# Splitting weights on GpSimd in smaller instructions, in one inference step of a diffusion backbone

## The chip, the cores and the metric

The kernel runs on one core of a Trainium2 chip. The metric is device time of one execution in microseconds, as the median over runs.

## What is computed

One step of a two-layer backbone over 128 context tokens and 512 latent tokens, 1024 channels, all in float32, with one set of weights. Cut to what matters here:

```python
def trunk(x, cond, states, is_context):
    for layer in range(DEPTH):                      # DEPTH = 2
        mod = jax.nn.silu(cond) @ w_ada[layer] + b_ada[layer]
        shift1, scale1, gate1, shift2, scale2, gate2 = jnp.split(mod[:, None, :], 6, axis=-1)
        h = rmsnorm(x, norm_mix_g[layer]) * (1 + scale1) + shift1
        if layer % 2 == 0:
            y, s_fin = mixer_ab(h, ...)             # gated DeltaNet || short gated conv, then @ w_out
        else:
            y = multiscale_pool(h, w_pool[o], pool_scale[o])
        x = x + gate1 * y
        h = rmsnorm(x, norm_ffn_g[layer]) * (1 + scale2) + shift2
        x = x + gate2 * conv_ffn(h, w_ffn_gate[layer], w_ffn_up[layer], ffn_conv[layer], w_ffn_down[layer])
    return rmsnorm(x, final_norm_g), finals

def conv_ffn(h, w_gate, w_up, conv, w_down):        # D_FF = 2816
    u = dwconv3(h @ w_gate, conv)
    return (jax.nn.silu(u) * (h @ w_up)) @ w_down
```

## The kernel before

All 640 tokens lie along the free axis and channels along the 128 partitions. A matrix product is done in units: one unit makes 128 output channels for all tokens, with 8 weight tiles of 128 x 128 (7 where a down group has 7 tiles of the hidden width, so 1024 or 896 columns of weights). Each float32 operand is split in a rounded part and a rest (`hi`, `lo`), and a unit multiplies three products, hi x hi, hi x lo and lo x hi, in 48 (or 42) matmuls of 320 columns (`products`, L942).

The weights of a unit arrive by DMA in `raw[s]`, s being the unit's number modulo 2. They are split in `whi[s]` (L758, a `tensor_scalar` by 1.0 plus 0.0 with rounded output) and `wlo[s]` (L761, a `tensor_tensor` subtraction, `raw` less `whi`). `split` does both on GpSimd: it waits for the load (`s_raw`) and until unit u - 2 is multiplied (`s_unit`), so it begins when TensorE turns to unit u - 1, and it tells TensorE by `s_split`. In the input projection VectorE and ScalarE split instead; in the up units of the first layer ScalarE rounds (L2094) and GpSimd only subtracts (`split_lo`, L766). The same two instructions stand written out for some units with buffers of their own: `first_hi`/`first_lo` (L864, L866), `third_hi`/`third_lo` (L897, L899), `mid_hi`/`mid_lo` (L853, L855), `last_hi`/`last_lo` (L910, L913). SyncE loads `raw[s]` again once `s_split` says that the unit in it is split.

The program goes: input projection (28 units), the DeltaNet scans, output projection (8 units), then for each layer three groups of the FFN, each with pairs of up units (gate and up, 8, 7 and 7 pairs) and 8 down units. The pooling mixer stands between the layers.

VectorE's work beside this is what the prediction speaks of. After an up pair's first unit, ScalarE copies the product (L2103), VectorE scales it (L2233) and adds two taps of the convolution in two ranges each (L2236, L2242); ScalarE applies silu (L2110); VectorE multiplies by the second unit's product, which it reads from PSUM (L2897); ScalarE rounds to `hidhi`, and VectorE subtracts to `hidlo` (L2900). In the down units and in the output projection VectorE updates x from PSUM (L2178, L2189) and, in the latter, adds squares (L2156). In between, in the first layer, in the output projection and in the second layer's first up group, it works off the modulation weights, rows of `w_ada`, two sums of 1024 columns for each row tile (`row_sums`, L2219; the tile `ada_raw`, outputs `junk` and `ada_raw`). TensorE waits for `hidlo` before a group's first down unit reaches the tile in question, and for the update of x before a pair of PSUM banks is written again.

The down group at the end of each layer is done in two halves of the tokens (L1392, L1523), with weights kept for both.

Of the kernel before, what the change touches and what calls it, by code (L numbers as in the profile page):

```python
# [61 lines left out]
SLOT = KD * P  # L62
PRIMED = 4

F32 = mybir.dt.float32
F32R = mybir.dt.float32r
ALU = mybir.AluOpType
# [90 lines left out]
def build(nc, t):  # L158
    ctx = ExitStack()
    with ctx:  # L160
# [9 lines left out]
        raw = [sb(f"raw{s}", [P, SLOT]) for s in range(2)]  # L170
# [579 lines left out]

        @block.gpsimd
        def _(pool):
            def split(u, half_u, s, n=SLOT, guard=True):
                pool.wait_ge(s_raw[s], half_u * 16 + 16)
                if guard:
                    pool.wait_ge(s_unit, u - 1)
                pool.sem_inc(s_go, 1)
                nc.gpsimd.tensor_scalar(whi[s][:, 0:n], raw[s][:, 0:n], 1.0, 0.0,  # L758
                                        ALU.mult, ALU.add).then_inc(s_whi, 1)
                pool.wait_ge(s_whi, u + 1)  # L760
                nc.gpsimd.tensor_tensor(wlo[s][:, 0:n], raw[s][:, 0:n], whi[s][:, 0:n].bitcast(F32),  # L761
                                        ALU.subtract).then_inc(s_split, 1)

            def split_lo(u, s):
                pool.wait_ge(s_whi, u + 1)
                nc.gpsimd.tensor_tensor(wlo[s][:], raw[s][:], whi[s][:].bitcast(F32),  # L766
                                        ALU.subtract).then_inc(s_split, 1)

            def split_lo_pairs(u, n_pairs, first=0):
                with pool.Fori(first, n_pairs) as i:  # L770
# [79 lines left out]
            def mid_split(m):  # L850

                pool.wait_ge(s_mid_raw[m], 16)
                nc.gpsimd.tensor_scalar(mid_hi[m][:], mid_raw[m][:], 1.0, 0.0, ALU.mult, ALU.add).then_inc(s_kept_hi, 1)  # L853
                pool.wait_ge(s_kept_hi, m - 1)
                nc.gpsimd.tensor_tensor(mid_lo[m][:], mid_raw[m][:], mid_hi[m][:].bitcast(F32),  # L855
                                        ALU.subtract).then_inc(s_kept_w, 1)

            for g, nf in enumerate(GROUPS):
                if g == 0:
                    u = SEG["up", 0, 0]["u"]  # L860
                    for j in range(2):
                        pool.wait_ge(s_raw[j], u // 2 * 16 + 16)
                        pool.wait_ge(s_unit, SEG["out"]["u"] + 2)
                        nc.gpsimd.tensor_scalar(first_hi[j][:], raw[j][:], 1.0, 0.0, ALU.mult, ALU.add).then_inc(s_whi, 1)  # L864
                        pool.wait_ge(s_whi, u + j + 1)
                        nc.gpsimd.tensor_tensor(first_lo[j][:], raw[j][:], first_hi[j][:].bitcast(F32),  # L866
                                                ALU.subtract).then_inc(s_split, 1)
                else:
                    split_pairs(SEG["up", 0, g]["u"], 1)
                if g == 2:  # L870
                    mid_split(2)
                u = SEG["up", 0, g]["u"] + 2
                if g == 0:
                    pool.wait_ge(s_raw[0], u // 2 * 16 + 16)
                    pool.wait_ge(s_unit, SEG["out"]["u"] + 7)
                    nc.gpsimd.tensor_scalar(whi[0][:], raw[0][:], 1.0, 0.0, ALU.mult, ALU.add).then_inc(s_whi, 1)
                    split_lo(u, 0)
                    split_lo(u + 1, 1)
                split_lo_pairs(u, nf, int(g == 0))
                if g < 2:  # L880
                    split_pairs(SEG["down", 0, g]["u"], 4, nf * P, first=1)
# [10 lines left out]
            for g, nf in enumerate(GROUPS[:2]):  # L892
                u = SEG["up", 1, g]["u"]
                if g == 0:
                    split_pairs(u, 1)
                    pool.wait_ge(s_raw[0], (u + 2) // 2 * 16 + 16)
                    nc.gpsimd.tensor_scalar(third_hi[:], raw[0][:], 1.0, 0.0, ALU.mult, ALU.add).then_inc(s_whi, 1)  # L897
                    pool.wait_ge(s_whi, u + 3)
                    nc.gpsimd.tensor_tensor(third_lo[:], raw[0][:], third_hi[:].bitcast(F32),  # L899
                                            ALU.subtract).then_inc(s_split, 1)  # L900
                    split(u + 3, (u + 2) // 2, 1)
                    split_pairs(u, nf, first=2)
                else:
                    split_pairs(u, nf)
                split_pairs(SEG["down", 1, g]["u"], 4, nf * P)

            def last_split(j):

                pool.wait_ge(s_last_raw, 16 * (KD - 2))
                nc.gpsimd.tensor_scalar(last_hi[j][:], last_raw[j - 2][:], 1.0, 0.0, ALU.mult, ALU.add)\  # L910
                    .then_inc(s_kept_hi, 1)
                pool.wait_ge(s_kept_hi, KEPT + j - 1)
                nc.gpsimd.tensor_tensor(last_lo[j][:], last_raw[j - 2][:], last_hi[j][:].bitcast(F32),  # L913
                                        ALU.subtract).then_inc(s_kept_w, 1)

            u = SEG["up", 1, 2]["u"]
            split_pairs(u, 3)
# [2179 lines left out]
```

## Time and profile before

| | |
|---|---|
| median of 3 runs | 1422.23 us (1421.07 to 1422.54) |
| the profiled execution | 1421.06 us |
| its span | 1419.3 us |
| TensorE (PE) busy | 1366.4 us, 96% |
| VectorE (DVE) busy | 989.5 us, 70% |
| ScalarE (ACT) busy | 412.9 us, 29% |
| GpSimd (POOL) busy | 517.7 us, 36% |
| GpSimd, L761 | 89 instructions, 229.4 us |
| GpSimd, L766 | 44 instructions, 112.5 us |
| GpSimd, L758 | 89 instructions, 95.8 us |

The span goes from the first to the last instruction. An instruction's time in a timeline runs from when its engine begins it to its end, and time in which it is held back inside counts as busy. So equal shapes with unequal durations are worth a look, and a busy share is not a share of work.

### The profile page before, as it was taken

The page shows a single profiled execution, that of the slowest core. Times are in us where ns is not written, and L with a number is a line of the kernel's source. Part 1 is how long each engine was busy: PE and PEld are TensorE (multiplying, and loading weights), DVE is VectorE, ACT ScalarE, POOL GpSimd, SP SyncE. Part 2 cuts the span into 40 slices and gives each one's busy share as a digit, 9 for nine tenths or more (in the row PEclk, how much of TensorE's full clock was granted, in tenths as well). Part 3 has the DMA queues.
Part 4 walks back from the last instruction along what each step waited for, and adds up shares of the span by engine and source line. Part 5 has one row for each costly group of instructions (what it writes and reads, how often), then busy time and mean ns, then how long its engine had stood idle before and what let it go on. Part 6 is the DMA issues. An engine that isn't in the chain of part 4 may idle for free.

```text
span 1419.3 us, 23699 instructions
## 1 busy us (share of the span) xinstructions
PE 1366.4 (96%) x9266; PEld 1331.6 (94%) x9266; DVE 989.5 (70%) x1474; ACT 412.9 (29%) x752; POOL 517.7 (36%) x315
## 2 busy tenths in 40 slices
PE   6999999989888999999999999999999999999997
PEld 4899899989778999999999999989999999999997
DVE  4887889858777877877788885688881355235554
ACT  4535344656026331023202232561110011001122
POOL 0000200141451334633465336215544455456650
PEclk9999999999999999999999999999999999999999
DMA  9645113432341453343354432112322224222202
GB/s 370 259 163 164 45 60 105 157 105 76 104 148 45 133 194 136 135 149 118 126 182 134 149 119 74 53 37 101 121 86 74 74 74 148 78 75 74 72 14 75
DMA packets 44718, 163.48 MB, mean 115 GB/s; under 512 B 4848, under 2 KB 7536, under 8 KB 42608
## 3 DMA queue, kind: packets, MB, share of 16 engines
q1 hardware_dynamic: 44656, 162.66, 33.1%
q8 instruction: 38, 0.62, 0.2%
q14 instruction: 24, 0.20, 0.0%
HBM read 154.26 MB, written 6.82 MB: 113 GB/s over the span
## 4 chain that ended last, share of the span: by engine, by line
PE 69%; DVE 13%; issue 10%; ACT 5%; POOL 2%; DMA 0%; DVEq 0%; ACTq 0%; SPq 0%; POOLq 0%
PE ps L942 52%; PE ps L1523 3%; PE ps L1392 3%; DVE junk L2219 2%; POOL wlo L766 2%; DVE ada_raw L2219 2%; DVE work L2236 1%; PE ps L1462 1%; PE ps L954 1%; DVE blocks L2435 1%; DVE outer L2432 1%; ACT work L1965 1%; PE ps L992 1%; PE ps L1086 1%; PE ps L1327 1%
## 5 line engine op out<-in xcount | busy, mean ns | idle before, releaser
L942 PE MATMUL ps<-hhi,whi 128*128 128x320 f32 x1824 | 419.3, 311 | 8.0 <-DVE x L2189 5.2
L942 PE MATMUL ps<-hlo,whi 128*128 128x320 f32 x1824 | 416.0, 309 | 0.0
L942 PE MATMUL ps<-hhi,wlo 128*128 128x320 f32 x1824 | 415.9, 309 | 0.0
L942 PEld LDWEIGHTS ps<-hhi,whi 128*128 128x128 f32 x1824 | 305.5, 188 | 12.2 <-DVE x L2189 6.0
L942 PEld LDWEIGHTS ps<-hlo,whi 128*128 128x128 f32 x1824 | 305.8, 188 | 0.0
L942 PEld LDWEIGHTS ps<-hhi,wlo 128*128 128x128 f32 x1824 | 305.7, 188 | 0.0
L761 POOL TENSOR_TENSOR wlo<-raw,whi 128x1024 fp32r<-128x1024 f32 (+1 forms) x89 | 229.4, 2578 | 7.4
L758 POOL TENSOR_SCALAR whi<-raw 128x1024 fp32r<-128x1024 f32 (+1 forms) x89 | 95.8, 1076 | 346.6 <-PE ps L942 272.6
L766 POOL TENSOR_TENSOR wlo<-raw,whi 128x1024 fp32r<-128x1024 f32 x44 | 112.5, 2558 | 208.7 <-ACT whi L2094 208.7
L2103 ACT ACTIVATE work<-ps 128x640 f32<-128x640 f32 x44 | 31.0, 704 | 380.3 <-PE ps L942 378.5
L2219 DVE SCALAR_TENSOR_TENSOR ada_raw<-ada_raw,cond_rows 128x1024 bf16<-128x1024 f32 x80 | 137.4, 1717 | 0.0
L2900 DVE TENSOR_TENSOR hidlo<-work,hidhi 128x640 fp32r<-128x640 f32 (+1 forms) x44 | 95.8, 2178 | 43.0 <-ACT hidhi L2115 43.0
L2219 DVE SCALAR_TENSOR_TENSOR junk<-ada_raw,cond_rows 128x1024 bf16<-128x1024 f32 x80 | 117.3, 1467 | 3.4 <-DMA ada_raw<-in_w_rows 1.0
L942 PE MATMUL ps<-hidhi,whi 128*128 128x320 f32 x480 | 110.1, 311 | 2.1 <-DVE hidlo L2900 2.1
L2236 DVE SCALAR_TENSOR_TENSOR work<-work,cols 128x511 f32<-128x511 f32 x120 | 109.3, 952 | 3.7 <-DVE work L2233 0.5
L2233 DVE TENSOR_SCALAR work<-work,cols 128x640 f32<-128x640 f32 x60 | 60.2, 1003 | 73.7 <-ACT work L2103 69.0
L942 PE MATMUL ps<-hidlo,whi 128*128 128x320 f32 x480 | 109.9, 310 | 0.0
L942 PE MATMUL ps<-hidhi,wlo 128*128 128x320 f32 x480 | 109.9, 310 | 0.0
L2110 ACT ACTIVATE work<-work 128x640 f32<-128x640 f32 x44 | 32.5, 739 | 265.5 <-DVE work L2242 265.5
L942 PEld LDWEIGHTS ps<-hidhi,whi 128*128 128x128 f32 x480 | 80.9, 189 | 2.4 <-DVE hidlo L2900 2.4
L942 PEld LDWEIGHTS ps<-hidlo,whi 128*128 128x128 f32 x480 | 80.9, 189 | 0.0
L942 PEld LDWEIGHTS ps<-hidhi,wlo 128*128 128x128 f32 x480 | 80.9, 189 | 0.0
(323 smaller groups left out, 1854.3 us busy)
## 6 DMA issues: line engine op xcount, KB each, us to landing
raw<-in_w_gu SPq DMA_DIRECT2D x88, 512.0 KB, 3.3
ada_raw<-in_w_rows SPq DMA_DIRECT2D x80, 512.0 KB, 3.4
raw<-in_w_in SPq DMA_DIRECT2D x28, 512.0 KB, 3.3
raw<-in_w_dn SPq DMA_DIRECT2D x24, 448.0 KB, 3.3
ada_first<-in_w_ada SPq DMA_DIRECT2D x8, 1024.0 KB, 18.3
raw<-in_w_dn SPq DMA_DIRECT2D x16, 512.0 KB, 3.5
raw<-in_w_out SPq DMA_DIRECT2D x8, 512.0 KB, 3.3
last_raw<-in_w_dn SPq DMA_DIRECT2D x6, 448.0 KB, 6.7
```

The costliest lines, as they stand in the source:

```text
L758: nc.gpsimd.tensor_scalar(whi[s][:, 0:n], raw[s][:, 0:n], 1.0, 0.0, ALU.mult, ALU.add).then_inc(s_whi, 1)
L761: nc.gpsimd.tensor_tensor(wlo[s][:, 0:n], raw[s][:, 0:n], whi[s][:, 0:n].bitcast(F32), ALU.subtract).then_inc(s_split, 1)
L766: nc.gpsimd.tensor_tensor(wlo[s][:], raw[s][:], whi[s][:].bitcast(F32), ALU.subtract).then_inc(s_split, 1)
L942: last = nc.tensor.matmul(pair[pr][:, b], wt[:, cs], act[:, k, b * HALF:(b + 1) * HALF], start=(first and j == 0 and q == 0), stop=(final ...
L1392: last = nc.tensor.matmul(mid_out(i)[:, 0:MID_SPANS[b][1] - MID_SPANS[b][0]], wt[:, cs], mid_of(act[:, j], b), start=(j == 0 and q == 0), ...
L1523: last = nc.tensor.matmul(pair["CB"[i % 2]][:, i // 2 % 2], wt[m][:, cs], half_of(act[:, j], b), start=(j == 0 and q == 0), stop=(j == LAS ...
L2103: nc.scalar.activation(halves(pad[0]), pair["A"], ACT.Copy).then_inc(s_ev["A"], 1)
L2110: nc.scalar.activation(cv[1], cv[0], ACT.Silu).then_inc(s_silu, 1)
L2219: last = nc.vector.scalar_tensor_tensor(out=(row_out(n), row_buf(n)[:, 0:SLOT // 2].bitcast(mybir.dt.bfloat16))[c], in0=row_buf(n), scalar ...
L2233: own.tick(nc.vector.tensor_scalar(dst[:, 0:W], src[:, 0:W], taps[1], None, ALU.mult))
L2236: last = nc.vector.scalar_tensor_tensor(out=dst[:, c0 + 1:c0 + n], in0=src[:, c0:c0 + n - 1], scalar=taps[0], in1=dst[:, c0 + 1:c0 + n], o ...
L2900: nc.vector.tensor_tensor(hidlo[:, i, :], h32[0], hidhi[:, i, :].bitcast(F32), ALU.subtract).then_inc(s_hid, 1)
```

## The change

Every rounding of weights on GpSimd is issued as two instructions over half the columns, and every subtraction as four over a quarter. The semaphore is raised by the last of them. Waits, buffers, the order of the work and all other engines stay as they are.

```diff
+            def round_parts(dst, src, n):
+
+                for c in range(0, n, n // 2):
+                    last = nc.gpsimd.tensor_scalar(dst[:, c:c + n // 2], src[:, c:c + n // 2], 1.0, 0.0, ALU.mult, ALU.add)
+                return last
+
+            def rest_parts(dst, src, hi, n):
+
+                for c in range(0, n, n // 4):
+                    cs = slice(c, c + n // 4)
+                    last = nc.gpsimd.tensor_tensor(dst[:, cs], src[:, cs], hi[:, cs].bitcast(F32), ALU.subtract)
+                return last
+
             def split(u, half_u, s, n=SLOT, guard=True):
                 pool.wait_ge(s_raw[s], half_u * 16 + 16)
                 if guard:
                     pool.wait_ge(s_unit, u - 1)
                 pool.sem_inc(s_go, 1)
-                nc.gpsimd.tensor_scalar(whi[s][:, 0:n], raw[s][:, 0:n], 1.0, 0.0,
-                                        ALU.mult, ALU.add).then_inc(s_whi, 1)
+                round_parts(whi[s], raw[s], n).then_inc(s_whi, 1)
                 pool.wait_ge(s_whi, u + 1)
-                nc.gpsimd.tensor_tensor(wlo[s][:, 0:n], raw[s][:, 0:n], whi[s][:, 0:n].bitcast(F32),
-                                        ALU.subtract).then_inc(s_split, 1)
+                rest_parts(wlo[s], raw[s], whi[s], n).then_inc(s_split, 1)
 
             def split_lo(u, s):
                 pool.wait_ge(s_whi, u + 1)
-                nc.gpsimd.tensor_tensor(wlo[s][:], raw[s][:], whi[s][:].bitcast(F32),
-                                        ALU.subtract).then_inc(s_split, 1)
+                rest_parts(wlo[s], raw[s], whi[s], SLOT).then_inc(s_split, 1)
...
```

The six places that have the instructions written out (L853 to L913) change in the same way.

On GpSimd, the loop over down units of 896 columns, before:

```order
L758 TENSOR_SCALAR whi<-raw 128x896
L760 REGISTER_ALU
L761 TENSOR_TENSOR wlo<-raw,whi 128x896
L756 REGISTER_ALU
L758 TENSOR_SCALAR whi<-raw 128x896
L760 REGISTER_ALU
L761 TENSOR_TENSOR wlo<-raw,whi 128x896
```

and with the change, whose lines are numbered anew:

```order
L756 TENSOR_SCALAR whi<-raw 128x448 x2
L772 REGISTER_ALU
L763 TENSOR_TENSOR wlo<-raw,whi 128x224 x4
L769 REGISTER_ALU
L756 TENSOR_SCALAR whi<-raw 128x448 x2
L772 REGISTER_ALU
L763 TENSOR_TENSOR wlo<-raw,whi 128x224 x4
```

Nothing moves: each instruction becomes two or four in its place, with nothing between the parts. The other engines' rows are the same but for their line numbers.

## Rows read from the trace of the kernel before

**Rows 1.** Table by stages: length; busy PE, PEld, DVE, ACT, POOL (count); clock; DMA.

```profile
445.00:848.00 403.00, 402.91 (x2745) 402.73 (x2746) 330.82 (x394) 88.04 (x109) 178.46 (x77) 1.00 0.41 140
```

**Rows 2.** Timeline of TensorE: start, us, what; in brackets idle before, and for whom.

```profile
366.36 0.41 PE L942 MATMUL ps<-hhi,whi 128*128 128x320 f32 x1 [0.35 <-POOL wlo L761]
...
408.06 0.39 PE L1327 MATMUL ps<-hhi,whi 128*128 128x320 f32 x1 [3.75 <-DVE x L2189]
...
850.43 0.42 PE L1392 MATMUL ps<-hidhi,whi 128*128 128x336 f32 x1 [0.85 <-POOL wlo L766]
...
931.80 0.33 PE L1438 MATMUL ps<-band,rows_tok 128*128 128x112 f32 x1 [0.86 <-DVE x L2807]
...
1060.05 0.47 PE L942 MATMUL ps<-hidhi,whi 128*128 128x320 f32 x1 [2.12 <-DVE hidlo L2900]
...
1361.78 0.41 PE L1523 MATMUL ps<-hidhi,whi 128*128 128x320 f32 x1 [0.73 <-POOL wlo L761]
```

**Rows 3.** Timelines: a GpSimd subtraction, a sum held by it, a sum alone.

```profile
367.89 3.24 POOL L761 TENSOR_TENSOR wlo<-raw,whi 128x1024 fp32r<-128x1024 f32 x1
...
368.81 3.41 DVE L2219 SCALAR_TENSOR_TENSOR ada_raw<-ada_raw,cond_rows 128x1024 bf16<-128x1024 f32 x1
...
1049.91 1.22 DVE L2219 SCALAR_TENSOR_TENSOR ada_raw<-ada_raw,cond_rows 128x1024 bf16<-128x1024 f32 x1
```

**Rows 4.** GpSimd with nobody in its way: timeline, and a group of lines (mean ns).

```profile
384.51 2.41 POOL L761 TENSOR_TENSOR wlo<-raw,whi 128x1024 fp32r<-128x1024 f32 x1
...
L913 POOL TENSOR_TENSOR last_lo<-last_raw,last_hi 128x896 fp32r<-128x896 f32 x6 | 12.8, 2128 | 0.5
...
1133.33 1.05 POOL L758 TENSOR_SCALAR whi<-raw 128x1024 fp32r<-128x1024 f32 x1 [3.49 <-PE ps L942]
...
1358.60 0.94 POOL L758 TENSOR_SCALAR whi<-raw 128x896 fp32r<-128x896 f32 x1 [3.64 <-issue]
```

**Rows 5.** Timelines about 279.8 us: a GpSimd row of small instructions, a VectorE copy.

```profile
277.72 2.45 POOL L807 TENSOR_SCALAR kg_p<-ktok,gates 128x128 f32<-128x128 f32 x7 [2.63 <-ACT ktok L1721]
...
279.81 0.64 DVE L2447 COPY work<-blocks 32x512 f32<-32x512 f32 x1
...
280.15 0.53 POOL L807 TENSOR_SCALAR kg_p<-ktok,gates 128x128 f32<-128x128 f32 x1
...
279.80 0.37 POOL L807 TENSOR_SCALAR kg_p<-ktok,gates 128x128 f32<-128x128 f32 x1
```

**Rows 6.** Timelines of one down unit of 896 columns, first layer.

```profile
723.82 0.94 POOL L758 TENSOR_SCALAR whi<-raw 128x896 fp32r<-128x896 f32 x1 [2.07 <-PE ps L942]
724.84 3.07 POOL L761 TENSOR_TENSOR wlo<-raw,whi 128x896 fp32r<-128x896 f32 x1
...
729.82 1.14 DVE L2189 SCALAR_TENSOR_TENSOR x<-ps,mod,x 128x320 f32<-128x320 f32 x3 [0.82 <-PE ps L942]
```

**Rows 7.** Timeline of VectorE at the end of the output projection.

```profile
403.48 3.37 DVE L2219 SCALAR_TENSOR_TENSOR ada_raw<-ada_raw,cond_rows 128x1024 bf16<-128x1024 f32 x1
```

**Rows 8.** Table by stages again, behind two waits of TensorE: the clock follows POOL.

```profile
375.80:379.20 3.40, 3.38 (x23) 3.39 (x24) 2.54 (x2) 0.74 (x1) 2.27 (x1) 1.00 0.57 178
...
1060.30:1063.70 3.40, 3.40 (x14) 3.40 (x14) 2.87 (x5) 0.00 (x0) 1.56 (x2) 0.50 0.00 0
```

**Rows 9.** Timeline of GpSimd in the pooling mixer.

```profile
921.33 2.36 POOL L899 TENSOR_TENSOR third_lo<-raw,third_hi 128x1024 fp32r<-128x1024 f32 x1
```

**Rows 10.** Timeline of VectorE in a pair of the second layer's first up group.

```profile
1045.10 1.55 DVE L2900 TENSOR_TENSOR hidlo<-work,hidhi 128x640 fp32r<-128x640 f32 x1 [0.90 <-ACT hidhi L2115]
1046.57 3.41 DVE L2219 SCALAR_TENSOR_TENSOR junk<-ada_raw,cond_rows 128x1024 bf16<-128x1024 f32 x1
...
1051.63 1.80 DVE L2236 SCALAR_TENSOR_TENSOR work<-work,cols 128x511 f32<-128x511 f32 x2
1053.46 2.85 DVE L2242 SCALAR_TENSOR_TENSOR work<-work,cols 128x511 f32<-128x511 f32 x1
```

**Rows 11.** Timeline of GpSimd before the last down projection.

```profile
1359.62 2.10 POOL L761 TENSOR_TENSOR wlo<-raw,whi 128x896 fp32r<-128x896 f32 x1
```

More of the change, by code:

```diff
@@ L852, in mid_split @@
                 pool.wait_ge(s_mid_raw[m], 16)
-                nc.gpsimd.tensor_scalar(mid_hi[m][:], mid_raw[m][:], 1.0, 0.0, ALU.mult, ALU.add).then_inc(s_kept_hi, 1)
+                round_parts(mid_hi[m], mid_raw[m], LAST).then_inc(s_kept_hi, 1)
                 pool.wait_ge(s_kept_hi, m - 1)
-                nc.gpsimd.tensor_tensor(mid_lo[m][:], mid_raw[m][:], mid_hi[m][:].bitcast(F32),
-                                        ALU.subtract).then_inc(s_kept_w, 1)
+                rest_parts(mid_lo[m], mid_raw[m], mid_hi[m], LAST).then_inc(s_kept_w, 1)
             for g, nf in enumerate(GROUPS):
@@ L863, in _ @@
                         pool.wait_ge(s_unit, SEG["out"]["u"] + 2)
-                        nc.gpsimd.tensor_scalar(first_hi[j][:], raw[j][:], 1.0, 0.0, ALU.mult, ALU.add).then_inc(s_whi, 1)
+                        round_parts(first_hi[j], raw[j], SLOT).then_inc(s_whi, 1)
                         pool.wait_ge(s_whi, u + j + 1)
-                        nc.gpsimd.tensor_tensor(first_lo[j][:], raw[j][:], first_hi[j][:].bitcast(F32),
-                                                ALU.subtract).then_inc(s_split, 1)
+                        rest_parts(first_lo[j], raw[j], first_hi[j], SLOT).then_inc(s_split, 1)
                 else:
@@ L875, in _ @@
                     pool.wait_ge(s_unit, SEG["out"]["u"] + 7)
-                    nc.gpsimd.tensor_scalar(whi[0][:], raw[0][:], 1.0, 0.0, ALU.mult, ALU.add).then_inc(s_whi, 1)
+                    round_parts(whi[0], raw[0], SLOT).then_inc(s_whi, 1)
                     split_lo(u, 0)
@@ L896, in _ @@
                     pool.wait_ge(s_raw[0], (u + 2) // 2 * 16 + 16)
-                    nc.gpsimd.tensor_scalar(third_hi[:], raw[0][:], 1.0, 0.0, ALU.mult, ALU.add).then_inc(s_whi, 1)
+                    round_parts(third_hi, raw[0], SLOT).then_inc(s_whi, 1)
                     pool.wait_ge(s_whi, u + 3)
-                    nc.gpsimd.tensor_tensor(third_lo[:], raw[0][:], third_hi[:].bitcast(F32),
-                                            ALU.subtract).then_inc(s_split, 1)
+                    rest_parts(third_lo, raw[0], third_hi, SLOT).then_inc(s_split, 1)
                     split(u + 3, (u + 2) // 2, 1)
@@ L909, in last_split @@
                 pool.wait_ge(s_last_raw, 16 * (KD - 2))
-                nc.gpsimd.tensor_scalar(last_hi[j][:], last_raw[j - 2][:], 1.0, 0.0, ALU.mult, ALU.add)\
+                round_parts(last_hi[j], last_raw[j - 2], LAST)\
                     .then_inc(s_kept_hi, 1)
                 pool.wait_ge(s_kept_hi, KEPT + j - 1)
-                nc.gpsimd.tensor_tensor(last_lo[j][:], last_raw[j - 2][:], last_hi[j][:].bitcast(F32),
-                                        ALU.subtract).then_inc(s_kept_w, 1)
+                rest_parts(last_lo[j], last_raw[j - 2], last_hi[j], LAST).then_inc(s_kept_w, 1)
             u = SEG["up", 1, 2]["u"]
```

## The prediction, made before the changed kernel had run

> **What bounds the kernel now.** I read the table by stages first, then TensorE's waits one by one in its timeline, then the timelines of GpSimd and VectorE at those places. TensorE is busy 402.91 of 403 us in the stretch from 445 to 848 [rows 1], and so again from 1063 to 1358. There a unit's weights are split while the unit before it multiplies, and a later or earlier split changes nothing until it misses TensorE's next unit. The change can act only where TensorE waits for the other two [rows 2]: for split weights (0.35 us at 366.36, 0.85 at 850.43, 0.73 at 1361.78), for VectorE's update of x (3.75 at 408.06, 0.86 at 931.80) and for the residue `hidlo` (2.12 at 1060.05).
>
> VectorE enters because it and GpSimd share something. One of its row sums takes 3.41 us and one 1.22 [rows 3]. The long one is asked for at 368.81, while GpSimd's subtraction runs until 371.13, and ends 1.1 later. GpSimd waits in turn: that subtraction takes 3.24 us against 2.41 alone [rows 3, 4], because a sum was still running when it was asked for. In all such places neither takes two turns while the other waits. The Trainium skill, "SBUF — State Buffer", section "Who interferes with whom", states the same: whichever issues second blocks until the first has finished. The trace agrees. Instructions with one operand in PSUM (the update of x, the product with `ps`) are not held. The change alters the length of GpSimd's turn and nothing else.
>
> **What a turn costs.** Subtractions that nobody holds take 2.41 us at 1024 columns and 2.13 at 896 [rows 4]: 0.28/128 = 2.2 ns a column and 0.16 us fixed. A quarter of 256 columns is 0.56 + 0.16 = 0.72 us. Roundings take 1.05 and 0.94 [rows 4]: 0.86 ns a column, 0.17 fixed; a half of 512 is 0.61. Seven GpSimd instructions in a row without waits take 2.45 us, one of them 0.37 [rows 5]: they start 0.35 apart, each 0.02 before the last ends. So two halves are 1.20 us and four quarters 2.80. With 0.08 between, a split grows from 3.54 to 4.08, by 0.54 us; of 896 columns by about 0.5; where ScalarE rounds (the first layer's up units) by 0.39. Bounds: below, only the time by columns, no growth; above, each of the four added instructions costs the whole 0.35 spacing of rows 5, 1.4 us a split. I take 0.54, from the same operations. The Trainium skill, "GPSIMD Engine Reference", section 3.1, gives 4497 ns for such an instruction of 2048 columns; with this trace's 2.41 us that makes, as an estimate, 0.84 us a quarter and one more microsecond a split, which is the third rival.
>
> **Do the parts let VectorE in?** Two engines meet among small instructions at 279.8 us [rows 5]: VectorE's copy of 279.81 takes 0.64 us, and the GpSimd instruction of 280.15, queued without a wait, takes 0.53 instead of 0.37. VectorE got in between two queued ones. It is one meeting, but the very case.
>
> **Part by part** (us, plus is slower).
>
> 1. The saturated stretches: 0. Down units of 896 columns are tightest [rows 6]: the split begins at 723.82 and the running unit ends where x is updated next, at 729.82. Turn by turn then: halves until 725.0, VectorE's first sum until 725.9, quarter 1, second sum until 727.5, quarters 2 to 4 until 729.3. It was ready at 727.91; 0.5 us of slack is left. A pair of up units in the first layer with four sums asks for two subtractions (5.6) and VectorE's turns (3.1 for convolution and `hidlo`, 4 x 1.15 for sums), 13.3 of the pair's 14.08 us. It fits.
>
> 2. Output projection: +0.4. The split that TensorE awaits at 366.36 [rows 2] becomes: halves, quarters 1 and 2, VectorE's add (0.7), quarter 3, a sum (1.1), quarter 4. With 0.54 of its own and these turns it ends 2.1 later. The next unit is held by an update of x anyway and starts within 0.1 of now; in the middle units VectorE sets the pace and loses about as much to short turns as to a long one. At the end, rounding and subtraction hold two sums until 406.85 [rows 7], and x comes at 407.9. Then: add, half, sum, half, sum until 404.8, x at 405.9, but the quarters, beside it and behind, end at 407.6: TensorE starts 0.4 earlier. With 0.1 from the unit before, -0.5. To this comes the clock. Behind the wait that ends at 1060.05 it is granted at 0.50, the 1.2 GHz level, for 3.4 us, which costs 1.7; behind the wait for x at 375.8 it stayed at 1.00 [rows 8]. The new 2.4 us wait at 366 may cost 1.7 or nothing: I count half, +0.9.
>
> 3. End of the first layer: +1.1. The subtraction that TensorE awaits at 850.43 [rows 2] has VectorE's `hidlo` behind it. Then: two quarters, `hidlo` (0.7), two quarters, in all 3.5 us instead of 2.4. The splits behind it grow by 0.5 each, which the slack they have now still covers.
>
> 4. Pooling mixer: +0.4. The last of three splits ends at 923.69 [rows 9]; with 0.54 each and more turns it will be 925.6, among VectorE's work that leads to the update awaited at 931.80. VectorE loses up to 1.1 there and has some of it to spare.
>
> 5. Second layer's first up group: -3.5, the main term. VectorE runs half a pair behind there. Per pair of 14.08 us it is held back 1.55 - 0.82, 3.41 - 1.22, 1.80 - 1.01 and 2.85 - 0.75, in all 5.8 us [rows 10], the second figure of each being the same shape with nobody in its way,, which is all that it could catch up: 14.08 less its own 8.3. With parts each of its 8 turns (scaling, four taps, `hidlo`, two sums) waits for one part at most, 0.6 us: 4.8 if GpSimd were always there, about 3.5 since it works 8.2 of 14.08. It gains 1 to 2.3 us a pair and is level before the 8 pairs end. The last `hidlo` no longer holds TensorE at 1060.05, 2.1 [rows 2], and the clock does not fall behind it, 1.7 [rows 8]. While VectorE catches up one split may be 0.3 late: -3.8 + 0.3. The turns add to 8.2 + 5.4 = 13.6 of 14.08, so they fit.
>
> 6. Last down projection: +1.1. The split that TensorE awaits at 1361.78 ends at 1361.72 [rows 11]. Then: halves from 1358.60 to 1359.7 [rows 4], two quarters, `hidlo`, two quarters, until 1362.8.
>
> Sum: 0 + 0.4 + 1.1 + 0.4 - 3.5 + 1.1 = -0.5. GpSimd's own work grows by about 100 x 0.54 + 44 x 0.39 = 71 us, hidden under TensorE as in 1; without that cover it would be the whole loss. Weight buffers come free at most 2 us later, with most of a 7 us unit to spare before the next load is awaited. The profiled execution took 1421.06 us, 1.17 below the median of the runs shown, 1422.23; so 1420.6 there, 1421.7 as median.
>
> **Rivals.** *The faster case.* Quarters cost 0.66 rather than 0.72 and no new clock fall comes: the projection gives -2.3, the two late splits +0.8 and +0.9, the mixer +0.2, item 5 -3.8: -4.2, 1418.0. For it speaks that rows 4 leave the fixed time open by that much. *Splits come too late.* If a quarter takes 0.15 more than I say, the turns make 13.6 + 1.8 = 15.4 of 14.08 in item 5 and 13.3 + 1.2 = 14.5 in the 13 up pairs with four sums: up to 1.3 and 0.4 us a pair, 9 + 5, of which half may show because turns don't always coincide, +7, and +3 more in the projection: 1432. It decides from about 0.08 more a quarter, when the 0.5 us of item 1 is gone. *The parts hold on.* If queued parts keep their turn, VectorE waits as long as now and 0.54 longer: +2 in the projection (four splits that hold it), +0.5, +0.5 and +0.3 at the other waits, item 5 as before: +3.3, 1425.5. Rows 5 speak against it.
>
> **How the numbers follow.** About 0.2% (2.8 us) is what a measurement can tell from no change. My forecast, inside that, 0.50; the faster case 0.22; late splits 0.15; parts that hold on 0.13, half of it over the bound. The rest of the spread is the clock's 1.7 either way. The range is 1417.5 to 1427: it takes in the faster case and the parts that hold on, and leaves out the far end of the late splits. Faster 0.23, within 0.2% 0.51, slower 0.26.
>
> **What would show it.** Right: VectorE's sums at 1.2 to 1.9 us and none at 3.4; `hidlo` near 1.4 us instead of 2.4; no wait at the first down unit of the second layer; waits for GpSimd's `wlo` of about 2 us in the projection and at the ends of both layers. Wrong: sums of 3 us (the parts hold on), waits for `wlo` inside the two saturated stretches (late splits), or quarters far from 0.72.

## The result and the profile after

| | before | changed |
|---|---|---|
| median | 1422.07 us (1420.97 to 1422.57, 6 runs) | 1430.07 us (1427.29 to 1432.62, 6 runs) |
| the profiled execution | 1421.06 us | 1432.62 us |
| TensorE busy | 1366.4 us | 1374.1 us |
| VectorE busy | 989.5 us | 888.1 us |
| GpSimd busy | 517.7 us | 718.5 us |

The changed kernel is slower, ratio 1.0058 (95% interval 1.0048 to 1.0068), by 8.0 us. I had forecast 1421.7 in 1417.5 to 1427: outside the range and on the other side. One execution of a variant below (the changed kernel with short sums, 2245.3 us, in a slow state) is left out of its median.

The profiled execution is the slowest of the six, 11.56 us over its counterpart of before. To see where they come from I compare the start of the same matmul in both traces. The last column is a second profiled execution of the changed kernel (1432.40 us, label changed_again below), given as its difference to before.

| same matmul starts at | before | changed | difference | added since the row above | again |
|---|---|---|---|---|---|
| end of the scans | 354.84 | 356.48 | 1.64 | 1.64 | 2.37 |
| end of the output projection | 444.38 | 447.82 | 3.44 | 1.80 | 4.78 |
| second pair of the first layer's first group | 472.95 | 480.66 | 7.71 | 4.27 | 9.08 |
| first layer's last up unit | 848.96 | 857.29 | 8.33 | 0.62 | 9.73 |
| its last down projection | 855.92 | 866.84 | 10.92 | 2.59 | 10.78 |
| behind the mixer | 962.00 | 972.94 | 10.94 | 0.02 | 10.75 |
| second layer's first group | 1035.91 | 1047.93 | 12.02 | 1.08 | 11.79 |
| its first down unit | 1064.92 | 1073.46 | 8.54 | -3.48 | 8.31 |
| last up unit | 1359.86 | 1368.74 | 8.88 | 0.34 | 8.66 |
| last down projection | 1370.98 | 1382.54 | 11.56 | 2.68 | 11.35 |

The first row is not the change's: GpSimd splits nothing there, and other kernels below, the same up to there, lie between -0.5 and +2.6. Much of it is the clock near 25 us, granted at 0.50 for 6.8 us in both profiles of the changed kernel and for 3.4 in that of before. The rest, some 9 to 10 us, is the change's.

The prices and the turns are as forecast. The groups of lines (count, then busy us and mean ns). First VectorE's in the kernel before, the row sums and `hidlo`:

```profile
L2219 DVE SCALAR_TENSOR_TENSOR ada_raw<-ada_raw,cond_rows 128x1024 bf16<-128x1024 f32 x80 | 137.4, 1717 | 0.0
L2900 DVE TENSOR_TENSOR hidlo<-work,hidhi 128x640 fp32r<-128x640 f32 (+1 forms) x44 | 95.8, 2178 | 43.0 <-ACT hidhi L2115 43.0
L2219 DVE SCALAR_TENSOR_TENSOR junk<-ada_raw,cond_rows 128x1024 bf16<-128x1024 f32 x80 | 117.3, 1467 | 3.4 <-DMA ada_raw<-in_w_rows 1.0
```

Then the changed kernel: GpSimd's parts, kept apart by shape, VectorE's sums, the larger of the two groups of `hidlo`, and from the timeline four quarters that nobody holds:

```profile
L763 POOL TENSOR_TENSOR wlo<-raw,whi 128x256 fp32r<-128x256 f32 x452 | 453.4, 1033 | 139.2 <-ACT whi L2100 133.3
L756 POOL TENSOR_SCALAR whi<-raw 128x512 fp32r<-128x512 f32 x140 | 92.2, 676 | 198.8 <-PE ps L948 142.1 <-PE ps L1468 26.8 <-DVE work L2795 26.7
L2225 DVE SCALAR_TENSOR_TENSOR junk<-ada_raw,cond_rows 128x1024 bf16<-128x1024 f32 x80 | 119.6, 1495 | 8.9 <-DMA ada_raw<-in_w_rows 6.5
L2225 DVE SCALAR_TENSOR_TENSOR ada_raw<-ada_raw,cond_rows 128x1024 bf16<-128x1024 f32 x80 | 121.8, 1523 | 0.0
L2906 DVE TENSOR_TENSOR hidlo<-work,hidhi 128x640 fp32r<-128x640 f32 x30 | 29.8, 993 | 27.5 <-ACT hidhi L2121 27.5
...
380.28 2.82 POOL L763 TENSOR_TENSOR wlo<-raw,whi 128x256 fp32r<-128x256 f32 x4
```

Four quarters alone take 2.82 us, 0.70 apart, but the mean quarter takes 1.03: many stand in line behind a VectorE instruction, up to 1.7 us each. So four quarters last 4 x 1.03 = 4.1 us where one subtraction took 2.6 on average (L761 and L766). Half of the 101 us that VectorE is busy less is `hidlo`, 1.0 us instead of 2.2. A sum takes 2.1 us at most instead of 3.4, but on average 1.5 instead of 1.6: before, 130 of 160 took 1.2 us, and now 55 do, since many wait for a quarter.

TensorE's waits, against [rows 2], which have 0.35, 3.75, 0.85, 0.86, 2.12 and 0.73 us:

```profile
370.17 0.89 PE L948 MATMUL ps<-hhi,whi 128*128 128x320 f32 x2 [2.47 <-POOL wlo L763]
...
389.50 0.56 PE L948 MATMUL ps<-hhi,whi 128*128 128x320 f32 x2 [3.67 <-DVE x L2195]
...
411.71 0.42 PE L1333 MATMUL ps<-hhi,whi 128*128 128x320 f32 x1 [2.73 <-POOL wlo L763]
...
458.53 0.63 PE L948 MATMUL ps<-hhi,whi 128*128 128x320 f32 x1 [2.70 <-POOL wlo L763]
...
859.81 0.42 PE L1398 MATMUL ps<-hidhi,whi 128*128 128x336 f32 x1 [1.90 <-POOL wlo L763]
...
942.72 0.64 PE L1444 MATMUL ps<-band,rows_tok 128*128 128x112 f32 x4 [1.32 <-DVE x L2813]
...
1371.82 0.41 PE L1529 MATMUL ps<-hidhi,whi 128*128 128x320 f32 x1 [1.89 <-POOL wlo L763]
```

The wait of 2.12 for `hidlo` is gone. Those at 370, 859 and 1371 are about as long as I had said. The one at 458 is new, and the one at 389 is longer than its predecessor of before. At several of them the clock fell. The table by stages (length; busy PE, PEld, DVE, ACT, POOL; clock):

```profile
369.70:373.10 3.40, 2.93 (x11) 2.94 (x12) 3.30 (x5) 0.00 (x0) 3.40 (x3) 0.50 0.49 154
...
390.20:393.60 3.40, 3.40 (x15) 3.40 (x14) 3.17 (x4) 0.20 (x1) 2.13 (x3) 0.50 0.68 265
...
458.50:461.90 3.40, 3.37 (x13) 3.38 (x14) 3.40 (x5) 0.00 (x0) 3.40 (x3) 0.50 0.64 229
861.20:864.60 3.40, 3.40 (x14) 3.40 (x13) 0.00 (x0) 0.00 (x0) 3.32 (x7) 0.50 0.54 162
1373.20:1376.60 3.40, 3.40 (x15) 3.40 (x14) 0.00 (x0) 0.00 (x0) 3.32 (x7) 0.50 0.00 0
```

Each of these falls lasts 3.4 us at 0.50, 1.2 GHz, and costs 1.7 where TensorE has work. The kernel before has falls too, near 357, 408, 937 and 1060 us. Behind the first row of the table above the changed kernel has seven, these five and two more near 359 and 428: three more than before, 5.1 us at most. The rest of its 9.9 us is longer waits, less the one that went.

### The profile page after: what moved, and what is told of

It reads as the page before. It is cut to its first block, busy times and chain, and to the rows that moved or that the text cites. A ratio compares the mean times of both kernels' runs of the same rounds, so it can differ in the third digit from the quotient of the medians.

```text
span 1430.8 us, 24240 instructions
## 1 busy us (share of the span) xinstructions
PE 1374.1 (96%) x9266; PEld 1337.1 (93%) x9266; DVE 888.1 (62%) x1474; ACT 414.2 (29%) x752; POOL 718.5 (50%) x856
## 4 chain that ended last, share of the span: by engine, by line
PE 76%; POOL 7%; DVE 7%; issue 6%; ACT 2%; DMA 1%; SPq 0%; POOLq 0%; DVEq 0%; ACTq 0%
PE ps L948 59%; POOL wlo L763 6%; PE ps L1529 3%; PE ps L1398 3%; PE ps L1428 1%; PE ps L960 1%; PE ps L998 1%; DVE blocks L2441 1%; DVE outer L2438 1%; POOL whi L756 1%; PE ps L1092 1%; PE ps L1062 1%; PE ps L1082 1%; DVE work L2836 1%; DVE wlo L2274 0%
## 5 line engine op out<-in xcount | busy, mean ns | idle before, releaser
L763 POOL TENSOR_TENSOR wlo<-raw,whi 128x256 fp32r<-128x256 f32 (+1 forms) x532 | 519.3, 1006 | 140.8 <-ACT whi L2100 133.3
L756 POOL TENSOR_SCALAR whi<-raw 128x512 fp32r<-128x512 f32 (+1 forms) x180 | 114.3, 653 | 236.7 <-PE ps L948 165.7
L2225 DVE SCALAR_TENSOR_TENSOR ada_raw<-ada_raw,cond_rows 128x1024 bf16<-128x1024 f32 x80 | 121.8, 1523 | 0.0
L2239 DVE TENSOR_SCALAR work<-work,cols 128x640 f32<-128x640 f32 x60 | 40.3, 672 | 111.3 <-ACT work L2109 106.8
L797 POOL TENSOR_TENSOR trig<-const,gates 128x512 f32<-128x512 f32 x10 | 12.5, 1262 | 176.7 <-DVE gates L2354 110.0
L2248 DVE SCALAR_TENSOR_TENSOR work<-work,cols 128x511 f32<-128x511 f32 x120 | 93.1, 815 | 3.6
L2242 DVE SCALAR_TENSOR_TENSOR work<-work,cols 128x511 f32<-128x511 f32 x120 | 91.6, 803 | 3.7 <-DVE work L2239 0.5
```

Of the source, the lines that this page charges most:

```text
L756: last = nc.gpsimd.tensor_scalar(dst[:, c:c + n // 2], src[:, c:c + n // 2], 1.0, 0.0, ALU.mult, ALU.add)
L763: last = nc.gpsimd.tensor_tensor(dst[:, cs], src[:, cs], hi[:, cs].bitcast(F32), ALU.subtract)
L2225: last = nc.vector.scalar_tensor_tensor(out=(row_out(n), row_buf(n)[:, 0:SLOT // 2].bitcast(mybir.dt.bfloat16))[c], in0=row_buf(n), scalar ...
L2239: own.tick(nc.vector.tensor_scalar(dst[:, 0:W], src[:, 0:W], taps[1], None, ALU.mult))
L2242: last = nc.vector.scalar_tensor_tensor(out=dst[:, c0 + 1:c0 + n], in0=src[:, c0:c0 + n - 1], scalar=taps[0], in1=dst[:, c0 + 1:c0 + n], o ...
L2248: last = nc.vector.scalar_tensor_tensor(out=dst[:, c0:c0 + n - 1], in0=src[:, c0 + 1:c0 + n], scalar=taps[2], in1=dst[:, c0:c0 + n - 1], o ...
```

## Experiments: one part alone

Every experiment is timed against the kernel before on the same chip. The differences in us are the ratio's distance from 1 times 1422, with its interval; they can be 1 us off the difference of the medians. The expectations give their rival theories letters. A is that a part waits for a VectorE turn, so that splits end later, which costs where TensorE waits for them; B that the parts' own fixed time is the loss; C that the clock alone is. The others are explained where they come. In the variants the two helpers take their numbers of parts from a list:

```diff
+            cut = [2, 4]
...
-                for c in range(0, n, n // 2):
+                for c in range(0, n, n // cut[0]):
...
-                for c in range(0, n, n // 4):
-                    cs = slice(c, c + n // 4)
+                for c in range(0, n, n // cut[1]):
+                    cs = slice(c, c + n // cut[1])
```

**Roundings alone** (`cut = [2, 1]`), **subtractions alone** (`cut = [1, 4]`):

> Roundings in two halves, subtractions whole. Theory A: a split ends later by 0.15 us plus at most one short VectorE turn, the long subtraction still holds VectorE, so the wait near 1060 stays: 0 to +3 us against before, with waits for wlo of 0.5 to 1.5 us more in the projection. Theory B (own time): 0.15 us at three or four waits, +0.5. Theory C: clock falls come at random, +0 to +3 with them in other places than those waits.

> Subtractions in four quarters, roundings whole. Theory A: three of the four added handovers are here, so nearly all of the change's loss and all of its gain: +4 to +8 us against before, with waits for wlo of 2 to 3 us in the projection and near 458, and none near 1060. Theory B (own time, 0.39 us at each wait): gain of the group less 1.5, so -1 to -2.5. Theory C: like the changed kernel without any pattern.

Roundings: 1418.11 us, -4.4 (-6.0 to -2.8), faster. Subtractions: 1428.76, +6.0 (+4.0 to +8.0). Theory A holds for the second and is wrong for the first: I had thought that the gain near 1060 needs a divided subtraction, and the trace has no wait there with roundings in halves either. B and C are out for the first as well, and B for the second. The two differences make +1.6, not +8.0, since both versions already have the gain near 1060 (between the table's rows 1035.91 and 1064.92 they win 3.9 and 3.8 us), and it can be had only once. So the roundings' halves cost next to nothing and suffice for the gain; the loss comes with the quarters.

**Other numbers of parts**, `cut = [1, 2]` and `cut = [4, 1]`:

> Subtractions in two halves, roundings whole: one handover where quarters have three. Theory A (the loss goes with the number of handovers, the gain near 1060 needs only one opening in GpSimd's sequence): no wait near 1060, waits for wlo of 0.7 to 1.5 us near 366, below 1.5 near 456, and 1.2 to 1.5 at the ends: -2 to +3 us against before. Theory B (own time): -3.5 to -2.5. Theory D (any opening in the subtraction costs as much as quarters, since the last part comes behind both sums anyway): +5 to +7.

> Roundings in four quarters, subtractions whole. Theory A: four openings where halves have two, each letting a VectorE instruction in ahead of the subtraction, which then ends later: the gain near 1060 stays (-3.8), the waits for wlo in the projection and the last down projection grow by 0.3 to 1.2 us each: -3 to +1 us against before, behind the version with halves (-4.0). If openings in the rounding are free: -3.5 or better.

Subtractions in halves: 1421.20, +0.4 (-0.9 to +1.7). Roundings in quarters: 1421.54, -0.4 (-1.7 to +0.9). Both lie in theory A's ranges. The second has the gain near 1060 and loses it again at the other waits; the first is there for a wrong reason: the wait near 1060 stayed. Its timeline:

```profile
1044.41 1.64 DVE L2907 TENSOR_TENSOR hidlo<-work,hidhi 128x640 fp32r<-128x640 f32 x1 [0.90 <-ACT hidhi L2122]
1045.97 2.30 DVE L2226 SCALAR_TENSOR_TENSOR junk<-ada_raw,cond_rows 128x1024 bf16<-128x1024 f32 x1
...
1059.37 0.68 PE L949 MATMUL ps<-hidhi,whi 128*128 128x320 f32 x2 [2.04 <-DVE hidlo L2907]
```

`hidlo` is held by the whole rounding, as in [rows 10], and then each sum by a half subtraction, 2.30 us: VectorE stays behind.

## Experiments: one place alone

**Only the second layer's first up group in parts** (`cut = [1, 1]` elsewhere), then the same group with **halves of the roundings alone**, then these and the output projection's:

```diff
+                    cut[:] = (2, 4)
                     split_pairs(u, nf, first=2)
+                    cut[:] = (1, 1)
```

> Parts only in the second layer's first up group (its units from the fifth on), every other split whole. Theory A (a part waits for a VectorE turn each time, so splits end later, which costs where TensorE waits for them, and more when the clock falls behind the longer wait; the gain is where VectorE lags): against the kernel before, -2.4 to -3.8 us, so 1418.3 to 1419.7; the wait near 1060 for hidlo and the clock fall behind it are gone, all other waits as before. Theory B (the parts' own fixed time is the loss, late splits everywhere, also under a busy TensorE): a loss inside the group of 0.5 us or more a pair that eats the gain, -1 to +3 us. Theory C (the loss is spread over the run by the clock alone, and the gain of this group too was the clock's): within 1 us of before.

> Roundings in halves in the second layer's first up group alone, all else whole. Theory G (one opening in the rounding lets VectorE pass it, so that it meets only the subtraction and catches up): the wait near 1060 and its clock fall are gone, no wait inside the group: -3.3 to -3.9 us against before, 1418.1 to 1418.8. Theory H (the gain of the version with all roundings in halves came from a VectorE that entered the group earlier, from cuts elsewhere): -1 to +1.

> Roundings in halves in the output projection and in the second layer's first up group, all else whole. Theory G, with the 0.65 us that halves gained in the projection, and without the 0.4 and 0.2 us that they cost in the mixer and the last down projection: -4 to -4.8 us against before, 1417.3 to 1418.1, at or ahead of the version with all roundings in halves. Theory H: -1.5 to +0.5.

All parts in the group: 1419.38, -2.4 (-3.7 to -1.1), the edge of theory A; in the trace it loses 1.6 within the group, 0.2 a pair and a wait of 0.49, and then gains 3.7. Roundings in halves in the group: 1418.02, -3.3 (-4.6 to -2.0); its trace has the same matmuls within 0.25 us of before until 1035.91, then 3.73 earlier at 1064.92: one place, 3.9 us, the 2.12 of the wait and the 1.7 of the clock. With the projection: 1416.94, -5.7 (-7.7 to -3.6). The medians are 4.6 apart, and the trace has 0.65 in the projection and 3.9 in the group, 4.6 too. It is the fastest, though its interval overlaps that of the group alone and of all roundings. Theory G holds; B, C and H are out. How VectorE gets past, in the version with halves in the group:

```profile
1002.61 0.83 DVE L2909 TENSOR_TENSOR hidlo<-work,hidhi 128x640 fp32r<-128x640 f32 x1 [0.90 <-ACT hidhi L2124]
...
1014.43 0.83 DVE L2909 TENSOR_TENSOR hidlo<-work,hidhi 128x640 fp32r<-128x640 f32 x1 [0.90 <-ACT hidhi L2124]
...
1025.61 2.75 DVE L2909 TENSOR_TENSOR hidlo<-work,hidhi 128x640 fp32r<-128x640 f32 x1 [0.90 <-ACT hidhi L2124]
```

`hidlo` comes at 1002.61, 11.8 us later, and 11.2 later: VectorE overtakes GpSimd. Before, every pair had its `hidlo` held by the rounding and its first sum by the subtraction [rows 10], and so took the 14.08 us of TensorE's pair however much VectorE could have done. An opening in the rounding breaks that step; once level, `hidlo` meets the subtraction (2.75 us), with time to spare.

With quarters the group loses first. One stretch of 95 us of the group in the changed kernel, of the same pairs before, and of the version with halves alone:

```profile
965.00:1060.00 95.00, 95.00 (x641) 93.75 (x640) 68.65 (x79) 15.30 (x21) 76.31 (x81) 1.00 0.31 105
```

```profile
954.00:1049.00 95.00, 95.00 (x650) 95.00 (x649) 82.21 (x74) 14.50 (x21) 51.86 (x27) 1.00 0.31 105
```

```profile
955.00:1050.00 95.00, 95.00 (x650) 95.00 (x649) 79.45 (x80) 15.13 (x21) 59.85 (x39) 1.00 0.32 106
```

TensorE is "busy" all 95 us in each, yet it starts 641 matmuls instead of 650, at equal clock. A matmul takes 403/2745 = 0.147 us [rows 1], so nine are 1.3 us. The busy time of its weight loads, 93.75 instead of 95.00, shows the same. The pairs come 14.30 us apart instead of 14.08 in the changed kernel, here by `hidlo` in two pairs, with GpSimd's split of the pair before them:

```profile
1051.52 1.09 DVE L2906 TENSOR_TENSOR hidlo<-work,hidhi 128x640 fp32r<-128x640 f32 x1 [0.90 <-ACT hidhi L2121]
...
1065.82 1.09 DVE L2906 TENSOR_TENSOR hidlo<-work,hidhi 128x640 fp32r<-128x640 f32 x1 [0.90 <-ACT hidhi L2121]
...
1036.89 5.38 POOL L763 TENSOR_TENSOR wlo<-raw,whi 128x256 fp32r<-128x256 f32 x4
```

One split in each pair, such as the one that ends at 1042.27, comes some 0.2 us after TensorE could have used it. A wait so short does not show as idle time; the counts show it.

**Whole where TensorE waits**, then the places one by one: the output projection whole, the first layer's first pairs whole (`cut[:] = (1, 1)` ahead of these splits and `(2, 4)` behind), the ends of both layers whole.

> Parts everywhere but in five places where TensorE waited for split weights: the output projection, the first pairs of the first layer's up group, the end of the first layer (last up pair and down units of its third group), and the first two units of the last down projection. Theory A: the loss is gone and the gain near 1060 stays, with 0.6 us left for splits just late in the stretches between: -1.5 to -3.5 us against before, 1418.6 to 1420.6. Theory B: only some of the loss goes, since about 100 of the 144 splits are still cut: +2 to +6. Theory C: as slow as the changed kernel, 1427 to 1431.

> The changed kernel with the output projection's splits whole again. Theory A (turns make the last part late; the clock falls behind the longer waits): the wait near 368 shrinks from 2.5 to 0.35 us, x is awaited 1.5 to 2.2 us instead of 3.7 near 386, up to three clock falls of 1.7 us go: 2.5 to 5 us less than the changed kernel, 1425 to 1427.5, so +3 to +5.5 against the kernel before. Theory B (own time only, 0.54 us a split): about 1 us less than the changed kernel, 1429.

> The changed kernel with whole splits from the first layer's first up units to the second pair of its first group (the subtraction that shares its time with the group's four row sums among them). Theory A: the wait of 2.7 us near 456 and the clock fall behind it are gone, so 3 to 5 us less than the changed kernel, 1425 to 1427, +3 to +5 against before; and in the profile that subtraction takes 2.9 us instead of four parts over 6.8 us. Theory B: the parts' own 0.39 us there costs at most that: 1429.5.

> The changed kernel once more, to have it in one batch with its variants. Six executions of it lay between 1427.3 and 1432.6. Theory A: the waits alone differ by about 5 us from before, and the rest is clock falls of 1.7 us each behind the new waits, whose number differs from execution to execution: executions again spread over 1427 to 1433 in steps of about 1.7, median 1428.5 to 1431. If the spread was chance of the first job: within 1 us of 1430.1.

> The changed kernel with whole splits at the ends of both layers (last up pair and down units of the first layer's third group, first two units of the last down projection). Theory A: the waits near 858 and 1370 shrink from 1.9 to 0.85 and 0.73 us, 2.2 together, and clock falls behind them go, 0 to 3.4: 2.2 to 5.6 us less than the changed kernel, 1424.5 to 1428. Theory B (own time only): 1.1 us less.

All of them: 1422.00, 0.0 (-1.3 to +1.3). The loss is gone, though not down to theory A's 1418.6 to 1420.6. Two things ate the gain: the pieces in the stretches between, and that I had left the first layer's second pair in quarters, behind which TensorE waited 0.51 and 0.81 us near 459 and 467.

One by one, against 1430.07 and 1430.22 (+8.2, +6.1 to +10.5) for the changed kernel: projection whole 1428.79 (+5.8, +3.8 to +7.7); first pairs whole 1425.93 (+4.1, +2.7 to +5.5); ends whole 1426.33 (+4.8, +3.0 to +6.7). The first pairs and the ends are in theory A's ranges, each worth 4 us. The projection is not: theory B's 1429 fits its median better. In the profiles it brings 3.1 to 3.7 us (the stretch from 354.84 to 444.38 takes 1.3 less than before instead of 1.80 or 2.41 more), between medians only 1.3 and between ratios 2.4. The 1.3 less is a clock fall near 357 us, which the profile of before has and this one lacks: from 363 us on the two go alike to the projection's end. So the parts cost the projection 1.8 us in the first profile of the changed kernel, which has that fall, and 3.7 in the second, which lacks it too. changed_again gives no verdict of its own: its median fits theory A and the other reading alike. Executions of the changed kernel spread over 6 us and those of this one over 6.5, so the places can't be added up to better than 2 us, and the projection's share stays open to that.

GpSimd where the first pairs are cut, before and changed, with what VectorE does between the parts:

```profile
449.56 2.40 POOL L766 TENSOR_TENSOR wlo<-raw,whi 128x1024 fp32r<-128x1024 f32 x1 [28.66 <-ACT whi L2094]
```

```profile
453.01 5.39 POOL L763 TENSOR_TENSOR wlo<-raw,whi 128x256 fp32r<-128x256 f32 x4 [27.34 <-ACT whi L2100]
...
453.64 0.83 DVE L2906 TENSOR_TENSOR hidlo<-work,hidhi 128x640 fp32r<-128x640 f32 x1 [0.81 <-ACT hidhi L2121]
454.39 1.76 DVE L2225 SCALAR_TENSOR_TENSOR junk<-ada_raw,cond_rows 128x1024 bf16<-128x1024 f32 x1
...
456.08 1.74 DVE L2225 SCALAR_TENSOR_TENSOR ada_raw<-ada_raw,cond_rows 128x1024 bf16<-128x1024 f32 x1
```

The split begins in both at the same point (453.01 less the 3.44 of the table is 449.57) and ends at 458.40 instead of 451.96 + 3.44 = 455.40. TensorE wanted it at 458.53 - 2.70 = 455.83: there were 0.4 us of slack, and the split takes 3.0 longer: 0.4 of its own, and 2.6 for `hidlo` and two sums between the quarters. Its next one, beside two more sums, is the one that waited 0.51 in whole_at_waits.

The ends, in whole_ends, with waits back at 0.85 and 0.73 and no fall of the clock behind either:

```profile
859.84 0.42 PE L1408 MATMUL ps<-hidhi,whi 128*128 128x336 f32 x1 [0.85 <-POOL wlo L764]
...
1369.14 0.42 PE L1539 MATMUL ps<-hidhi,whi 128*128 128x320 f32 x1 [0.73 <-POOL wlo L764]
```

## Experiments: the turns and the row tile

**Short sums.** Both kernels with the row sums over 64 columns; their modulation rows are sums over these columns alone.

```diff
-                        in1=cond_rows[:, c, :],
+                        in1=cond_rows[:, c, 0:64],
```

and likewise `[:, 0:64]` for the output and `in0`.

> The kernel before with VectorE's row sums taken over 64 of 1024 columns (the modulation rows are then not the reference's), so that a sum is a turn of about 0.2 us instead of 1.2. Both theories: VectorE is no longer late near 1060, that wait and its clock fall are gone, -2 to -6 us against the kernel before.

> The changed kernel with the same short row sums. Theory A (lateness comes from waiting for VectorE's turns): against the kernel before with short sums only +1.5 to +4.5 us, since only the turns of the add, the taps and hidlo are left: no wait near 456, 0.5 to 1.3 us more near 368, still 1 us more at the ends of both layers, perhaps with clock falls. Theory B (the parts' own fixed time, and clock falls without a cause there): still +7 to +9, the whole difference, with the wait near 456.

1406.79 and 1415.48 us: the change still costs 8.7 between medians, 8.0 between ratios. The first expectation has the wait near 1060 gone, which is so, but the time fell by 15.2, not 2 to 6: in the projection, too, the sums were on the path, 10.9 us in the trace. The second was wrong in its number, which lies in theory B's range. I had not counted that with short sums the gain near 1060 has nothing left to gain. In the traces the loss without that gain is 11.56 - 1.64 + 3.48 = 13.4 us with long sums and 9.0 - 0.8 = 8.2 with short ones; so 5.2 us go with the sums. Of them 1.5 is the last down projection, where no sum runs and a clock fall came with long sums and not with short ones; so the sums' turns and what hangs on them make 4 us or less, and the rest comes from other turns and the clock. By place: the loss within the second layer's first group is gone, and the wait at 458 shrinks from 2.70 to

```profile
446.56 0.55 PE L948 MATMUL ps<-hhi,whi 128*128 128x320 f32 x2 [0.74 <-POOL wlo L763]
...
845.72 0.42 PE L1398 MATMUL ps<-hidhi,whi 128*128 128x336 f32 x1 [1.90 <-POOL wlo L763]
```

and the one at the first layer's end, where no sum runs but `hidlo`, stays at 1.90. That is theory A by place; theory B would have left the first as it was. What the 0.74 still consists of isn't shown.

**The row tile.** SyncE's queue in the projection, before (first fence) and changed (second, with VectorE); then GpSimd in the changed kernel:

```profile
366.25 5.24 SPq L588 DMA_DIRECT2D raw<-in_w_out  x2
372.25 0.33 SPq L593 DMA_DIRECT2D ada_raw<-in_w_rows  x1
```

```profile
370.05 7.19 SPq L588 DMA_DIRECT2D raw<-in_w_out  x2
377.28 0.91 SPq L593 DMA_DIRECT2D ada_raw<-in_w_rows  x2
...
383.13 1.23 DVE L2225 SCALAR_TENSOR_TENSOR junk<-ada_raw,cond_rows 128x1024 bf16<-128x1024 f32 x1 [5.57 <-DMA ada_raw<-in_w_rows]
```

```profile
370.00 3.13 POOL L756 TENSOR_SCALAR whi<-raw 128x512 fp32r<-128x512 f32 x2
373.22 3.67 POOL L763 TENSOR_TENSOR wlo<-raw,whi 128x256 fp32r<-128x256 f32 x4
```

The row tile's load stands behind a weight load that waits for the second split. That split ended at 371.13 [rows 3] and now ends at 376.89, since its halves and its first quarter each waited for a sum. The tile is asked for 5.0 us later, VectorE stands idle 5.57 us, and x comes at 389.5. I issued one row tile's load ahead of that weight load, in the changed kernel and in the one before:

```diff
-            for k, n in ((4, 0), (5, 4), (6, 2), (7, 0)):
+            for k, n in ((4, 1), (5, 3), (6, 2), (7, 0)):
```

> The changed kernel with one row tile's load in the output projection issued ahead of the weight load that waits for the late split. Theory E (the late split holds the row tile on SyncE's queue, and the row sums hold the update of x): VectorE no longer waits 5.6 us near 378, TensorE waits 1.5 to 3 us for x near 386 instead of 3.7 to 6.2: 2 to 4 us less than the changed kernel, 1426 to 1428.5. Theory F (VectorE's turns with GpSimd's parts alone make x late): within 1 us of 1430.2.

> The kernel before with the same row tile's load issued earlier. Both theories: the tile was there in time, within 1 us of 1422; a weight load that is late by less than 2 us costs nothing.

Changed: 1428.04 us, +7.3 (+5.3 to +9.1); control: 1421.86, -0.6 (-1.8 to +0.7), no difference. So 2.0 us less than the changed kernel between medians, the low end of theory E, but 0.9 between ratios, which theory F would allow. The times don't decide; the profile shows that the queue held the tile, and its projection takes 0.8 longer than before instead of 1.8 and 2.4. First a profile of the changed kernel (changed_again), then this one:

```profile
389.93 0.63 PE L948 MATMUL ps<-hhi,whi 128*128 128x320 f32 x1 [6.23 <-DVE x L2195]
```

```profile
369.43 0.33 SPq L593 DMA_DIRECT2D ada_raw<-in_w_rows  x1
...
375.79 1.21 DVE L2225 SCALAR_TENSOR_TENSOR junk<-ada_raw,cond_rows 128x1024 bf16<-128x1024 f32 x1
...
381.85 1.23 DVE L2225 SCALAR_TENSOR_TENSOR junk<-ada_raw,cond_rows 128x1024 bf16<-128x1024 f32 x1 [3.29 <-DMA ada_raw<-in_w_rows]
...
385.33 0.41 PE L948 MATMUL ps<-hhi,whi 128*128 128x320 f32 x1 [2.53 <-DVE x L2195]
```

The sums that started at 383.13 start at 375.79 (1.7 of it is the earlier start of that profile), the next tile is still awaited 3.29 us, and TensorE starts at 385.33 instead of 389.93, of which 2.4 are that profile's later start.

## Why the prediction was wrong

The mechanism was right: the turns go from part to part, quarters cost about the 0.72 that I had said (0.70 apart), VectorE's waits shrink, splits end later, and the wait near 1060 goes. The sum was wrong, -0.5 where the traces show 9 to 10 and the medians 8.0. By its own steps:

1. *The saturated stretches, 0*: failed, +4.3, +0.6 and +0.3 us. I took the tightest case to be a down unit with 0.5 us to spare, which came out as worked (that split ends at 737.19, and the unit at 737.70), and checked up pairs by their mean load, 13.3 of 14.08 us. The second split of the first layer's first pair isn't a mean: ScalarE's rounding comes late there, it had 0.4 us to spare, and it grew by 3.0. This step, with its clock fall, is half the loss; making it whole gave back 4 us.
2. *Output projection, +0.4*: 1.8 and 2.4 in the two profiles (3.7 in the second if one allows for the fall that it lacks). The split awaited there was right (2.4 us of wait forecast, 2.47 measured), and so was the sign at its end (3.75 to 2.73), but that gave nothing: in the same profile TensorE then waits 2.84 us at 426.47 for `hlo`, the rest of the normalized x, where its longest wait for it was 1.5 before. Wrong was the sentence that the next unit "starts within 0.1 of now" and that weight buffers that come free 2 us later cost nothing: in SyncE's queue a row tile that VectorE needs stands behind the weight load, and was asked for 5.0 us later.
3. *End of the first layer, +1.1*: the wait grew by 1.05 (0.85 to 1.90). The clock fall behind it, 1.7, was put at nothing, without a reason. It came in one of two profiles of the changed kernel.
4. *Pooling mixer, +0.4*: the wait for x grew by 0.46, to 1.32, but the matmul behind it starts at 942.72 instead of 931.80, 10.92 later, and 10.92 was the difference at the first layer's end already: nothing was added.
5. *Second layer's first up group, -3.5*: measured -3.48 at its end, as forecast, after a loss of 1.08 within the group, -2.4. Failed here is "the turns add to 13.6 of 14.08, so they fit": the pairs take 14.30. Its "about 3.5" does not follow either: 4.8 x 8.2/14.08 is 2.8. And the reason was too broad. I wanted parts everywhere, but one opening in the rounding is enough; in the subtraction one is not, three are.
6. *Last down projection, +1.1*: the wait grew by 1.16, and the clock fell behind it in both profiles, again put at nothing: +2.7 in all.

So two steps failed and carry the miss: "saturated stretches: 0", for a place with hardly any slack (4.3), and clock falls (1.7 each) behind waits that grew from below 0.9 to about 1.9, which I counted once, by half, in the projection and nowhere else. The rival of late splits, 1432, was nearest in time. It rested on dearer quarters, which is not what happened, so its number is luck; its other sign, waits for `wlo` inside the saturated stretches, is what the profile shows.

## What to carry to other kernels

Cutting an instruction that holds a shared resource helps the engine that waits and delays the one that is cut by up to one turn for each part, so count parts times the neighbour's turn, at the place where the neighbour queues most, not in the mean. Cut where the neighbour is caught every time and nobody awaits the result closely: here halves of the rounding in two places gave 4.6 us by medians and trace, and all parts everywhere cost 8. And follow a late result through every in-order queue behind it, and look at the count of matmuls in a stretch, not at their busy share, to see waits below 0.3 us.

## What the runs showed of the hardware beyond that

- A clock fall behind a wait isn't certain. Behind 1.90 us at the end of the first layer it came in the first profile of the changed kernel (above) and not in the second, nor in three variants with the same wait (whole_in_proj, whole_first_pairs, changed_row_earlier). Behind 1.89 us at the last down projection it came in both profiles and in the first two of these variants, and not in the third. The second profile at the first place:

```profile
862.60:866.00 3.40, 3.40 (x24) 3.40 (x23) 1.04 (x2) 0.66 (x2) 3.32 (x6) 1.00 0.52 179
```

- In the projection a fall was hidden by the wait behind it. The first profile had one from 369.7, and then waited 3.67 us for x; the second had none, arrived sooner and waited 6.23. TensorE went on at 389.50 and 389.93.
- Executions of the changed kernel spread over 6 us (1426.7 to 1432.6 in twelve), those of the kernel with halves in one group over 2.3 (eleven), and those of the kernel before over 3.4 to 6.9 in the four batches of 17 to 23. Which falls come in an unprofiled execution can't be seen; that they make this spread is argued, not shown.
